# Router logits from the residual sums instead of the normed rows, in a two-layer decoder trunk with experts

## The reference

```python
x = layer_norm(DN_ALPHA * x + f(x), g, b)

# hierarchical_moe, on the x that ln_xa has normed
g_logits = xf @ wg + bg                      # 4 groups
g_star = argmax(g_logits)
e_logits = (einsum('td,dge->tge', xf, we) + be)[g_star]   # 8 experts of the best group
top_val, top_idx = top_k(e_logits, 2)
gate = softmax(g_logits)[g_star] * softmax(top_val)
# y += gate * (silu(x @ w1[e]) * (x @ w3[e])) @ w2[e] for the two experts
```

## Time and profile before

| | |
|---|---|
| median of 3 runs | 1376.88 us (1374.98 to 1380.55) |
| profiled execution | 1377.9 us, span in the profile 1376.1 us |
| busy: PE, PEld, DVE, ACT, POOL | 1142.7, 735.4, 393.5, 165.3, 30.5 us |
| granted TensorE clock, mean | 0.926 |
| read from HBM | 473.58 MB, 346 GB/s over the span; 428 GB/s in the slices from about 310 to 690 us and again from about 960 us |
| layer 0: projection ends, first expert | 278.2 us, 291.4 us |
| layer 1: the same | 911.0 us, 924.1 us |

### The profile page before, as it was taken

One profiled execution on the slowest core, in us unless ns is written; L12 is line 12 of the kernel. 1 busy time (PEld: TensorE's weight loads), 2 busy tenths in 40 slices (PEclk: granted clock), 3 DMA queues, 4 the chain that ended last, 5 costly groups with the idle time before them and its releaser, 6 DMA issues.

```text
span 1376.1 us, 30241 instructions
## 1 busy us (share of the span) xinstructions
PE 1142.7 (83%) x11896; PEld 735.4 (53%) x11897; DVE 393.5 (29%) x1032; ACT 165.3 (12%) x462; POOL 30.5 (2%) x85
## 2 busy tenths in 40 slices
PE   8999999997996776768799999999896766766656
PEld 7885658554554344335458867655453433434333
DVE  1972632351331221212232133253231111111213
ACT  1112502110110000000010001111110000000001
POOL 3000000000000000000000000000000000000001
PEclk9999999998998898888999999999998888888888
DMA  9856059579999999999997657555999999999996
GB/s 347 253 184 245 1 179 370 216 308 428 428 428 430 428 429 427 431 428 428 428 409 276 245 200 324 204 220 202 425 428 428 430 428 427 429 428 430 427 429 273
DMA packets 69241, 477.39 MB, mean 347 GB/s; under 512 B 8460, under 2 KB 13868, under 8 KB 43852
## 3 DMA queue, kind: packets, MB, share of 16 engines
q1 hardware_dynamic: 67148, 470.27, 83.3%
q0 software_dynamic: 2048, 6.47, 1.4%
HBM read 473.58 MB, written 3.15 MB: 346 GB/s over the span
## 4 chain that ended last, share of the span: by engine, by line
PE 58%; DMA 31%; SPq 6%; issue 3%; another core or an unknown queue 1%; DVE 1%; ACT 0%; POOL 0%; DVEq 0%
DMA ring<-in_moe_w_dram 21%; PE bank L1073 13%; PE bank L588 12%; DMA slot<-in_moe_w_dram 10%; PE bank L611 8%; SPq L500 5%; PE bank L1091 4%; PE bank L1099 3%; PE bank L1056 2%; PE bank L596 2%; PE bank L797 2%; PE bank L957 1%; PE bank L975 1%; PE bank L645 1%
## 5 line engine op out<-in xcount | busy, mean ns | idle before, releaser
L1073 PE MATMUL bank<-ring,xT 128*32 128x256 f32 x1920 | 174.5, 447 | 40.1 <-DMA ring<-in_moe_w_dram 40.1
L1634 DVE SCALAR_TENSOR_TENSOR xT<-xT,bank 64x256 f32<-64x256 f32 x73 | 30.3, 415 | 491.8 <-ACT xT L1900 491.7
L1073 PE MATMUL bank<-slot,xT 128*32 128x256 f32 x1120 | 167.4, 465 | 2.9 <-issue 2.9
L1073 PE MATMUL bank<-held,xT 128*32 128x256 f32 x608 | 93.8, 470 | 57.3 <-DMA slot<-in_moe_w_dram 48.6
L588 PE MATMUL bank<-xT,ring 128*128 128x256 f32 x640 | 139.9, 379 | 0.7 <-PE bank L588 0.7
L1073 PEld LDWEIGHTS bank<-ring,xT 128*32 128x32 f32 x1920 | 89.9, 128 | 80.3 <-issue 60.0
L588 PEld LDWEIGHTS bank<-xT,ring 128*128 128x128 f32 x640 | 121.1, 190 | 17.3 <-issue 1.1
L1073 PE MATMUL bank<-spare,xT 128*32 128x256 f32 x512 | 76.7, 466 | 46.2 <-DMA ring<-in_moe_w_dram 45.0
L611 PE MATMUL bank<-ring,slot 128*128 128x512 f32 x256 | 111.4, 593 | 0.7 <-PE bank L588 0.7
L1073 PE MATMUL bank<-gains,xT 128*32 128x256 f32 x512 | 75.3, 459 | 42.2 <-DMA slot<-in_moe_w_dram 42.2
L1091 PE MATMUL bank<-ring,xT 128*32 128x256 f32 x1824 | 108.9, 379 | 0.0
(11 more groups left out here) (292 smaller groups left out, 1113.3 us busy)
## 6 DMA issues: line engine op xcount, KB each, us to landing
ring<-in_moe_w_dram SPq DMA_DIRECT2D x94, 2048.0 KB, 47.2
slot<-in_moe_w_dram SPq DMA_DIRECT2D x44, 2048.0 KB, 48.8
held<-in_moe_w_dram SPq DMA_DIRECT2D x16, 2048.0 KB, 41.3
spare<-in_moe_w_dram SPq DMA_DIRECT2D x14, 2048.0 KB, 47.0
gains<-in_moe_w_dram SPq DMA_DIRECT2D x14, 2048.0 KB, 47.1
ring<-in_od_w_in_dram SPq DMA_DIRECT2D x6, 2048.0 KB, 21.3
ring<-in_xa_wq_dram SPq DMA_DIRECT2D x4, 2048.0 KB, 11.4
ring<-in_xa_wo_dram SPq DMA_DIRECT2D x4, 2048.0 KB, 12.7
```

Of the source, the lines that this page charges most:

```text
L1073: ins = mm(b1[qs[2 * m + h], 0:S], xg[:, k, :], ws[m][:, k, h, :, :], start=(k == 0), stop=(k == KC - 1))
L1634: stt(out=glu, in0=th, scalar=1.0, in1=banks[5][0:P // 2, 0:S], op0=ALU.add, op1=ALU.mult).then_inc(fam.glu_done, 1)
```

## The change

The router's logits are computed from the transposed residual sums. Once, in layer 0, VectorE multiplies `wr` of both layers by the gain and sums it over the blocks, and does the same for the norm's bias; TensorE sums over the rows with a matrix of ones (`router_sums`, between the first and second half of the first output projection), ScalarE copies the sums, VectorE subtracts the column means (`centre_router`, ahead of the norm behind layer 0's cross-attention) and adds the constant to `rbias`, which now lies on 128 rows. In each layer the transposes wait for the sums alone, xT is written by plain copies of 128 x 512 (three by ScalarE, one by VectorE), each routing begins with logits * rstd + constant, and x is normed in two passes, (x - mean) * gain and then times rstd plus bias. Fillers go. Norms of the mixers and behind the experts stay as they are.

```diff
-        rbias = sb("rbias", [1, DEPTH, RW])
-        lg = sb("lg", [P, TT, NG, EPG])
+        rbias = sb("rbias", [P, DEPTH, RW])
+        lg = sb("lg", [P, TT, RW])
...
             def normal(i, t):
-                if i % 3 == 2:
+                if i % 3 == 1:
+                    for h in range(2):
+                        wait_drained(pe, ("f", i, t, h))
+                elif i % 3 == 2:
...
+            def router_sums():
+                n = DEPTH * RW
+                ps = claim(pe, ("fold",), bank=MIXED)
+                pe.wait_ge(wr_sums, 1)
+                mm(ps[:, 0:n], ones[:, :], gain_sums.rearrange("p l n -> p (l n)"), start=True, stop=True)
+                filled(mm(ps[:, n:2 * n], ones[:, :], shift_sums[:, :, :].rearrange("p l n -> p (l n)"), start=True, stop=True), ("fold",))
...
-                def logits(t, warm=0):
-                    pe.wait_ge(router_loaded, 16 * 2 * DEPTH)
-                    ps = claim(pe, ("lg", L, t), bank=(None, 5)[t])
-                    keep_warm(ps, warm)
-                    pe.wait_ge(bias_loaded, 32)
-                    mm(ps[:, 0:RW], ones[0:1, :], rbias[0:1, L, :], start=True, stop=False)
-                    for k in AS_TURNED:
-                        fresh_part(3 * L + 1, k, t)
-                        ins = mm(ps[:, 0:RW], xT[:, k, t * P:(t + 1) * P], wr[:, L, k, :], start=False, stop=(k == 3))
-                    filled(ins, ("lg", L, t))
-                logits(0)
-                turned(("n", 3 * L + 1), x, 1, 5)
-                logits(1, 2)
+                def logits(t, h):
+                    if h == 0:
+                        claim(pe, ("lg", L, t), bank=(None, 5)[t])
+                    wait_drained(pe, (("n", 3 * L + 1), t, h))
+                    ps = banks[bank_of[("lg", L, t)][0]]
+                    for k in range(4 * h, 4 * h + 4):
+                        ins = mm(ps[:, 0:RW], xT[:, k, t * P:(t + 1) * P], wr[:, L, k, :], start=(k == 0), stop=(k == KC - 1))
+                    if h == 1:
+                        filled(ins, ("lg", L, t))
+                pe.wait_ge(wr_centred, DEPTH)
+                logits(0, 0)
+                turned(("n", 3 * L + 1), x, 1)
+                logits(0, 1)
+                logits(1, 0)
+                logits(1, 1)
...
+        def minus_mean(st, v, i, t):
+            v.wait_ge(gb_loaded, 32 * (i + 1))
+            for h in range(2):
+                wait_filled(v, (("n", i), t, h))
+            v.wait_ge(ln_stats, 2 * i + t + 1)
+            return st.mark(nc.vector.scalar_tensor_tensor(out=x[:, t, :], in0=x[:, t, :], scalar=mv[:, t, 0:1], in1=gb[:, 0, :],
+                                                          op0=ALU.subtract, op1=ALU.mult))
+        def by_rstd(st, v, i, t, at_):
+            st.wait(at_)
+            v.wait_ge(ln_rstd, 2 * i + t + 1)
+            nc.vector.scalar_tensor_tensor(out=x[:, t, :], in0=x[:, t, :], scalar=rstd[:, t, :], in1=gb[:, 1, :],
+                                           op0=ALU.mult, op1=ALU.add).then_inc(x_ready[t], 1)
...
+            for L in range(DEPTH):
+                row = lngT[:, 3 * L + 1, :, :]
+                st.do(tt(shifted, wr[:, L, :, :], row[:, 1, :].unsqueeze(2).to_broadcast([P, KC, RW]), ALU.mult))
+                st.mark(tt(wr[:, L, :, :], wr[:, L, :, :], row[:, 0, :].unsqueeze(2).to_broadcast([P, KC, RW]), ALU.mult))
+                st.mark(nc.vector.tensor_reduce(shift_sums[:, L, :], shifted.rearrange("p k n -> p n k"), AX, ALU.add))
+                st.wait()
+                st.do(nc.vector.tensor_reduce(gain_sums[:, L, :], wr[:, L, :, :].rearrange("p k n -> p n k"), AX, ALU.add))
+            v.sem_inc(wr_sums, 1)
+            def centre_router():
+                wait_drained(v, ("fold",))
+                v.wait_ge(bias_loaded, 32)
+                for L in range(DEPTH):
+                    stt(out=wr[:, L, :, :], in0=gain_sums[:, L, :].unsqueeze(1).to_broadcast([P, KC, RW]), scalar=-1.0 / D,
+                        in1=wr[:, L, :, :], op0=ALU.mult, op1=ALU.add).then_inc(wr_centred, 1)
+                st.do(tt(rbias[:, :, :], rbias[:, :, :], shift_sums[:, :, :], ALU.add))
...
                 def best_group(t):
                     ps = wait_filled(v, ("lg", L, t))
-                    st.do(nc.vector.max(top[:, t, 0, :], ps[:, 0:RG]))
-                    st.do(nc.vector.max_index(topi[:, t, 0, :], top[:, t, 0, :], ps[:, 0:RG]))
+                    v.wait_ge(ln_rstd, 2 * (3 * L + 1) + t + 1)
+                    drained(stt(out=lg[:, t, :], in0=ps[:, 0:RW], scalar=rstd[:, t, :], in1=rbias[:, L, :], op0=ALU.mult, op1=ALU.add), ("lg", L, t))
+                    wait_drained(v, ("lg", L, t))
+                    st.do(nc.vector.max(top[:, t, 0, :], lg[:, t, 0:RG]))
+                    st.do(nc.vector.max_index(topi[:, t, 0, :], top[:, t, 0, :], lg[:, t, 0:RG]))
...
-                norm_dve(st, v, 3 * L + 1, first_tile)
-                two_experts(0)
-                multiplied = gain(st, v, 3 * L + 1, 1)
-                best_group(1)
-                one_group(1)
-                two_best(1)
-                two_experts(1)
-                gain_bias(st, v, 3 * L + 1, 1, multiplied)
+                i = 3 * L + 1
+                norm_stats(st, v, i, 0, 0)
+                norm_stats(st, v, i, 0, 1)
+                st.wait()
+                row_rstd(v, i, 0, 2)
+                norm_stats(st, v, i, 1, 0)
+                ps = wait_filled(v, (("n", i), 0, 1))
+                drained(cp(xT[:, 4:KC, 0:P], ps[:, :].rearrange("p (k s) -> p k s", k=4)), (("n", i), 0, 1))
+                by_rstd(st, v, i, 0, minus_mean(st, v, i, 0))
+                norm_stats(st, v, i, 1, 1)
+                st.wait()
+                row_rstd(v, i, 1, 2)
+                at_ = minus_mean(st, v, i, 1)
+                route(0)
+                route(1)
+                by_rstd(st, v, i, 1, at_)
...
-                norm_act(a, 3 * L + 1)
+                for t, h in ((0, 0), (1, 0), (1, 1)):
+                    key = (("n", 3 * L + 1), t, h)
+                    ps = wait_filled(a, key)
+                    drained(cp(xT[:, 4 * h:4 * h + 4, t * P:(t + 1) * P], ps[:, :].rearrange("p (k s) -> p k s", k=4)), key)
...
-            g.dma_start(rbias[:, :, 0:NG], T["moe_bg"].unsqueeze(0)).then_inc(bias_loaded, 16)
+            g.dma_start(rbias[:, :, 0:NG], T["moe_bg"].unsqueeze(0).to_broadcast([P, DEPTH, NG])).then_inc(bias_loaded, 16)
```

More of the change, by code:

```diff
@@ L249, in program @@
         n_ready = sem("n_ready")
+        wr_sums = sem("wr_sums")
+        wr_centred = sem("wr_centred")
         row_scale = [sem(f"row_scale{t}") for t in range(TT)]
@@ L571, in fresh_part @@
                 if c < 3:
-                    pe.wait_ge((xT_by_act, xT_by_dve)[h], 3 * (TT * i + t) + c + 1)
+                    pe.wait_ge((xT_by_act, xT_by_dve)[h], 3 * (TT * (i - (i + 1) // 3) + t) + c + 1)
                 else:
@@ L597, in by_tile, with out_projection @@
                 return ins
-            def out_projection(name, i, ready):
+            def out_projection(name, i, ready, between=None):
                 ws = []
@@ L612, in out_projection @@
                         filled(ins, ("f", i, t, h))
+                        if between is not None and t + h == 0:
+                            between()
                         if t == 1 and h == 0:
@@ L919, in _ @@
                         wait_drained(pe, ("mv", t, h))
-                out_projection(f"wo_mix{L}", 3 * L, (mixed_first, mixed_second)[L])
+                out_projection(f"wo_mix{L}", 3 * L, (mixed_first, mixed_second)[L], router_sums if L == 0 else None)
                 if L == 0:
@@ L1208, in to_xT, with norm_stats, norm_dve @@
             drained(ins, (("n", i), t, 1))
-        def norm_dve(st, v, i, behind=None):
+        def norm_stats(st, v, i, t, h):
+            if i and h == 0:
+                v.wait_ge(x_ready[t], i)
+            key = ("f", i, t, h)
+            ps = wait_filled(v, key)
+            xx = x[:, t, h * 512:(h + 1) * 512]
+            drained(nc.vector.scalar_tensor_tensor(out=xx, in0=xx, scalar=ALPHA, in1=ps[:, :], op0=ALU.mult, op1=ALU.add), key)
+            wait_drained(v, key)
+            st.mark(nc.vector.bn_stats(out=bn[:, t, h, :], in_=xx))
+        def minus_mean(st, v, i, t):
[10 more added lines that the diff above has]
+                                           op0=ALU.mult, op1=ALU.add).then_inc(x_ready[t], 1)
+        def norm_dve(st, v, i):
             if i == 0:
                 v.wait_ge(small_loaded, 16 * 8)
-            def stats(t, h):
-                if i and h == 0:
-                    v.wait_ge(x_ready[t], i)
-                key = ("f", i, t, h)
-                ps = wait_filled(v, key)
-                xx = x[:, t, h * 512:(h + 1) * 512]
-                drained(nc.vector.scalar_tensor_tensor(out=xx, in0=xx, scalar=ALPHA, in1=ps[:, :], op0=ALU.mult, op1=ALU.add), key)
-                wait_drained(v, key)
```

(13 more changed lines are left out.)

45 lines of the change are left out of this document (22 added, 23 removed).

## The result

The changed kernel takes 1378.39 us in the median of 13 runs (1377.37 to 1382.31), the kernel before 1376.88, of 13 runs too: ratio 1.0017, 95% interval 1.0009 to 1.0025. That is 0.17% slower where 0.3% faster was forecast, and inside the range. The profiled execution took 1378.08 us with a span of 1376.3, against 1377.9 and 1376.1 before.

A forecast was written before the change was run, and what follows sets the result against it. VectorE's path to expert 0 was taken to bound the experts' start, with a saturated weight stream behind. Two layers, -4.4, plus 0.5 for column sums gave -3.9: median 1373.0 us against 1376.88, range 1369.5 to 1379.0.

The forecast's parts named there:

- the whole is kept: Experts' start, both layers: gains' transfer and expert 0 move with `place`, and the weight stream keeps all 2.2 us, -4.4 together.
- a reload at 14.8 instead of 17.0: Sign in the profile after: first reload of an expert's slot comes 14.8 us behind the sums instead of 17.0.
- `place` 2.2 us earlier: VectorE's path from tile 1's sums through routing: `place` starts at 286.6 against 288.83, 2.2 us earlier per layer.
- the bound of 1.7: Low end of the gain of `place` per layer, 1.7 to 3.1 us, with x passes and small instructions at their bounds.
- Folding, centring and the sums: Ahead of layer 0's norms: folding about 4 us and centring at most 2.1, both hidden on VectorE; TensorE's column sums cost +0.5.
- The fillers "at nothing": Seven filler products of 512 columns leave TensorE at no cost, because it waits there anyway; no clock loss is counted.
- rival 1: Clock falls before expert 0 starts, through narrow products: +2.9 against -2.2 per layer; both layers 1378.8, one 1375.9; chance 0.17.
- a clock of 0.5 around expert 0: Sign of being wrong: a granted clock of 0.5 around expert 0, where 1.00 up to expert 0 was expected.
- rival 3: Unexplained stalls, 2.03 us at 296.53 in layer 0: one may vanish, 1371.0, or appear in layer 1, 1375.0; chance 0.12.
- rival 2: Earlier start is hidden in a layer by a late preload or another wait: one layer lost 1375.2, both 1377.4; chance 0.10.
- the empty window at 294: No DMA transfers at 294 to 296 us in layer 0, held as evidence against the earlier start being hidden.
- Rival 4: Folded matrix rounds otherwise, a near tie changes expert, and the count of 32-row rounds changes by one, some 7.6 us; chance 0.03.

The follow-up runs named there:

- its three variants: Kernel before with 64 empty instructions at TensorE's start, 1376.59 us; with the last preload late, 1379.62; with another 1 MB preload held back in layer 1, 1377.35.

## Why the prediction was wrong, point by point

**The step that failed is "the whole is kept", for layer 1.** The prediction let `place` carry expert 0, expert 0 the reloads, and the reloads the rest. The last preload moves with them, and TensorE's instructions wait behind it. In layer 1 the sum up to the first reload is 1.55 gained, then 2.18 lost to the gap, 0.09 in small shifts and 1.64 to the clock: +2.36, which is 28.49 less 26.13. At the end of the span +2.1 is left of it, 467.19 less 465.12. The prediction's sign for the whole, a reload at 14.8 instead of 17.0, was read from layer 0 alone; the reload of layer 1 before, at 26.13, stood in none of its rows. The last part is 464.96 to 465.49 in the kernel before and its three variants, and 466.89 to 467.53 in the changed kernel with the gap left as it is (four profiles). With the preload held back in layer 1 alone or in both layers, and the gap unfilled there, it is 463.60 to 464.60.

**"The whole is kept" in layer 0** stands for the start of the stream: the held reload is 15.46 to 15.48 us behind the sums in all kernels with the change but the one with the transposes first, 16.99 before. The stream's third transfer, behind the gap and the lower clock, is 25.35 behind the sums against 24.61 before. How much of 1.5 reached the end isn't settled. The medians leave about a microsecond (+1.5 in all, less 2.1 of layer 1 and 0.4 of the sums gives -1.0), and single profiles of f0 to f1 spread by up to 3.1 for one code of layer 0.

**`place` 2.2 us earlier: mis-sized, 1.55.** `place` is at 9.02 instead of the worked-out 8.35. The first pass over x starts 0.52 late (2.47 instead of 1.95 behind the sums), 0.40 of it because the prediction had the transposes follow the sum by 0.06, but tile 0's logits stand ahead. 0.14 is the routing, 2.08 a tile (914.86 less 912.78) against 2.01: the new instruction took 0.25, near the taken 0.22. The passes over x, taken at 1.22, took 1.28 and 1.27, and 1.20 and 1.19 from start to start. Nothing was wrong in kind, and 1.55 is just below the bound of 1.7, because the bounds varied the durations and not the order.

**Folding, centring and the sums** held. The kernel after on VectorE and TensorE, ahead of layer 0's first norm:

```profile
169.99 0.48 DVE L1568 TENSOR_TENSOR slot<-wr,lngT 128x320 f32<-128x320 f32 x1
170.91 0.76 DVE L1570 TENSOR_REDUCE lg<-slot 128x40 f32<-128x320 f32 x1
...
174.25 0.77 DVE L1572 TENSOR_REDUCE e<-wr 128x40 f32<-128x320 f32 x1
...
180.27 0.69 DVE L1236 SCALAR_TENSOR_TENSOR x<-x,bank 128x512 f32<-128x512 f32 x1 [5.25 <-PE bank L618]
```

```profile
180.00 0.34 PE L897 MATMUL bank<-e,ones 128*128 128x80 f32 x2
...
180.41 13.94 PE L618 MATMUL bank<-ring,slot 128*128 128x512 f32 x32
```

Folding took 5.0 us (169.99 to about 175.0), in cover, with 5.25 idle left; the prediction had "about 4 likelier" under a bound of 5.5. The sums cost 0.41 (180.00 to 180.41) against 0.5.

**The fillers "at nothing"** held up to expert 0, where the clock stayed at 1.00. It fell behind expert 0, in both layers, a place for which the sum and rival 1 have no price; a clock of 0.5 around expert 0 was one of the prediction's own signs of being wrong. It didn't fall for want of the old fillers: in layer 1 it stays at 1.00 without them once the gap is short (0.22 to 0.50 us), and new fillers in the gap cure it.

**The rivals.** What came is rival 3's "may appear in layer 1" with the cause that rival 2 names, a preload, and the price of rival 1, whose 1378.8 is near the measured 1378.39 by coincidence: it had the clock fall ahead of expert 0 by way of narrow products, and knew of no gap. Each stood alone, with chances of 0.12, 0.10 and 0.17. Rival 2 looked for a preload that lands too late, and the one that counted was too early. Its own "against", the empty window at 294, asked only whether weights were moving, not whether instructions were. Nor do the transfers stay away from this place, as the prediction read from its windows at 268 and 294: from 917 to 919 us the kernel before moves 422 GB/s. Rival 3 had the row in hand, 2.03 us of "issue" at 296.53, and took it for noise that could come or go; moving the preload in the kernel before lengthened it (2.03 to 3.57), so it is the same wait. Rival 4 didn't occur: ScalarE's waits for a hidden product, one a round, number 73 in both kernels.

**What stays open.** The trace has no record of when the block is asked for, so why it is asked for earlier, against the work, in layer 1 than in layer 0 was not found. Why the clock fell behind 1.75 us of waiting and not behind 2.03 is open too. That the preload's time makes the gap of layer 1 is shown. That the block is TensorE's and carries the delay is argued, from the scatter that follows it by 4.2 to 4.3 us in the five profiles with an early preload and by 4.4 to 4.9 in layer 0 of all.

## What to carry to other kernels

When an edit moves an engine's work forward, list every transfer whose issue moves with it and ask what small thing queues behind each, instruction blocks among them; an idle stretch put down to "issue" is the place to look, and the DMA view by queue, in windows of a quarter microsecond, says when the block landed. A wait with no releaser in the kernel before is a cost with a cause, not noise: it should be explained before a chance is put on it. And a reading that a sum rests on, here the reload that follows `place`, has to be made in every layer to which the sum is applied. Here the remedy was one wait in one layer that holds a preload back until the block is through, and it turned a loss of 0.17% into a gain of 0.15%.

## What was not expected of the hardware

- A 16 KB block of instructions landed with the last packets of a 1 MB transfer issued ahead of it, 4.3 to 4.5 us behind that transfer's issue, in five profiles (the kernel after, with gap fillers, with 64 and with 40 empty instructions, and the kernel before with a moved transfer). In the kernel after run again it came at 3.8 us, some packets sooner.
- Behind 2.18 us without work the granted clock was 0.54 at 929 to 932 us; with eight products of 512 columns (1.89 us) in the gap it was 1.00. Behind 2.03 us without work in layer 0 of the kernel before it was 1.00 as well, behind 2.35 us in the same place of its variant with a moved transfer 0.50, and behind 1.75 us in layer 1 of the changed kernel run again 0.81 at 930 to 932 us.
- The clock also fell with TensorE on record as busy: 0.50 at 284 us behind 3.66 us of 40-column products, and 0.51 at 138 us in the earlier trace rows. It doesn't do so each time: the same 3.66 us in layer 1 of that kernel were followed by 1.00.
- A reduction of 320 strided elements to 40 takes 0.76 us, where the product of the same 320 takes 0.48; three operands over 1024 columns take 1.28 where two took 1.22.
